# A routed-expert kernel whose router picks experts by eight-largest and index search and gathers tile by tile

## The reference

```python
g_logits = xt @ w_rg + b_rg                       # 4 groups
g_sel = jnp.argmax(g_logits, axis=-1)
e_logits = (xt @ w_re + b_re).reshape(T, 4, 8)    # 8 experts in each group
e_sel = e_logits[chosen group]
top_p, top_i = lax.top_k(softmax(e_sel), 2)       # two experts per token
y = sum over the two experts of  weight * (silu(xt @ w_gate[e]) * (xt @ w_up[e])) @ w_down[e]
```

## Time and profile before

| | us |
|---|---|
| median of 3 runs | 1901.54 |
| lowest and highest run | 1900.3, 1905.17 |
| profiled execution: span from first to last instruction | 1899.8 |
| PE matmul busy | 1538.8 (81%) |
| DVE busy | 424.5 (22%) |
| ACT busy | 248.6 (13%) |
| POOL busy | 86.5 (5%) |
| read from memory | 708.17 MB, 373 GB/s over the span |

### The profile page before, as it was taken

One profiled execution on the slowest core, in us unless ns is written; L12 is line 12 of the kernel. 1 busy time (PEld: TensorE's weight loads), 2 busy tenths in 40 slices (PEclk: granted clock), 3 DMA queues, 4 the chain that ended last, 5 costly groups with the idle time before them and its releaser, 6 DMA issues.

```text
span 1899.8 us, 23382 instructions
## 1 busy us (share of the span) xinstructions
PE 1538.8 (81%) x10250; PEld 744.4 (39%) x10250; DVE 424.5 (22%) x940; ACT 248.6 (13%) x531; POOL 86.5 (5%) x142
## 2 busy tenths in 40 slices
PE   8999777999998778989977677776799667677776
PEld 4654433764454434445522212221355222222222
DVE  3341011326431213464500000000043000000001
ACT  0410000126212011154100000000011000000000
POOL 1100000201100000112100000000000000000000
PEclk9999888999999999999998878888899888788888
DMA  7579999769979999299699999999988999999997
GB/s 289 208 283 423 422 423 417 285 251 388 352 301 417 420 421 413 92 364 381 262 424 424 424 424 423 424 424 424 420 336 333 424 423 423 423 424 424 423 423 293
DMA packets 132110, 711.11 MB, mean 374 GB/s; under 512 B 8376, under 2 KB 13480, under 8 KB 67488
## 3 DMA queue, kind: packets, MB, share of 16 engines
q1 hardware_dynamic: 125584, 697.14, 90.0%
q0 software_dynamic: 4320, 9.78, 1.5%
q10 hardware_dynamic: 2096, 2.57, 0.4%
HBM read 708.17 MB, written 1.05 MB: 373 GB/s over the span
## 4 chain that ended last, share of the span: by engine, by line
PE 45%; DMA 43%; DVE 5%; SPq 2%; issue 2%; ACT 2%; POOL 1%; DVEq 0%; PEldq 0%; ACTq 0%; POOLq 0%
DMA ring<-in_moe_w 25%; DMA ring<-in_moe_w_down 6%; PE pa L824 5%; DMA work<-in_moe_w 5%; PE pb L795 4%; PE pa L842 4%; DMA mod<-in_moe_w 3%; PE acc L897 3%; PE pb L772 3%; PE acc L1425 3%; PE acc L1420 2%; PE pb L750 2%; SPq L706 2%; PE acc L1143 2%; PE acc L1321 2%; DMA ring<-in_moe_w_up 2%
## 5 line engine op out<-in xcount | busy, mean ns | idle before, releaser
L795 PE MATMUL pb<-ring,XT 128*32 128x512 f32 x1296 | 263.1, 742 | 89.5 <-DMA ring<-in_moe_w 89.5
L824 PE MATMUL pa<-ring,work 128*32 128x512 f32 x928 | 182.9, 723 | 71.4 <-DMA ring<-in_moe_w 45.7
L795 PEld LDWEIGHTS pb<-ring,XT 128*32 128x32 f32 x1296 | 59.2, 130 | 242.6 <-DMA ring<-in_moe_w 130.0
L943 DVE TENSOR_TENSOR work<-work,pb 128x256 f32<-128x256 f32 (+1 forms) x32 | 17.7, 554 | 585.5 <-PE pb L795 412.6
L897 PE MATMUL acc<-XT,work 128*128 128x512 f32 x256 | 118.4, 605 | 32.5 <-DVE XT L959 19.6
L842 PE MATMUL pa<-work,HM 128*128 128x128 f32 x1024 | 127.5, 286 | 15.5 <-issue 15.5
L842 PEld LDWEIGHTS pa<-work,HM 128*128 128x128 f32 x1024 | 126.1, 202 | 30.2 <-issue 30.2
L795 PE MATMUL pb<-work,XT 128*32 128x512 f32 x416 | 106.3, 713 | 28.3 <-DMA work<-in_moe_w 28.3
L772 PE MATMUL pb<-ring,XT 128*32 128x256 f32 x1472 | 102.9, 399 | 13.6 <-DMA ring<-in_moe_w_up 13.6
L824 PEld LDWEIGHTS pa<-ring,work 128*32 128x32 f32 x928 | 40.4, 128 | 177.0 <-issue 75.7
L906 ACT COPY XT<-pa 128x512 f32<-128x512 f32 x32 | 18.8, 586 | 588.6 <-PE pa L842 588.6
(11 more groups left out here) (417 smaller groups left out, 1834.5 us busy)
## 6 DMA issues: line engine op xcount, KB each, us to landing
ring<-in_moe_w SPq DMA_DIRECT2D x135, 2048.0 KB
work<-in_moe_w SPq DMA_DIRECT2D x46, 2048.0 KB
ring<-in_moe_w_up SPq DMA_DIRECT2D x28, 2048.0 KB
ring<-in_moe_w_gate SPq DMA_DIRECT2D x26, 2048.0 KB
ring<-in_moe_w_down SPq DMA_DIRECT2D x24, 2048.0 KB
ring<-in_w_mod SPq DMA_DIRECT2D x48, 1024.0 KB
mod<-in_moe_w SPq DMA_DIRECT2D x11, 2048.0 KB
work<-in_moe_w_down SPq DMA_DIRECT2D x8, 2048.0 KB
```

The lines of the kernel that those rows point to most:

```text
L795: last = nc.tensor.matmul(hbank[m][j * CAP:(j + 1) * CAP, :], m_xg[:, k, j * CAP:(j + 1) * CAP], slot_of(s0 + j // 2)[:, at:at + fn], star ...
L824: last = nc.tensor.matmul(pa[j * CAP:(j + 1) * CAP, h, :], m_ht[:, c, j * CAP:(j + 1) * CAP], slot_of(i)[:, at:at + 512], start=(c == 0), ...
```

## The change

In the router each tile's choice takes `max` (the eight largest of a row, in order) and `max_index` (their positions): once for the group, on 8 columns of which 4 are padding of -3e30, and once for the two experts. The logits' columns change places (experts first, then groups). The order of work changes: after tile 0's choice PE computes its ranks, DVE its slots, and PE gathers tile 0 for round 0 while DVE chooses for tile 1; then come tile 1's ranks and slots, and round 0 starts with the second half of its gather. The expert counts are summed after that. Ten warming matmuls before the ranks and four behind become four before each tile's ranks. Tile 1's residual (`carry_tensor(pe, ph, 1)`) moves from behind the logits into round 0, between gate and up and the wait for `hh`. A semaphore of the second mixer is folded into another.

```diff
-            for lo, hi, n in ((0, NG, "g"), (NG, NG + NE, "e")):
+            if ph.moe:
+                pool.wait_ge(assign_ready, TT * ph.moe)
+            for lo, hi, n in ((NE, NE + NG, "g"), (0, NE, "e")):
...
-            carry_tensor(pe, ph, 1)
-            warm_tensor(pe, pb[:, 0, :], 10)
-            pe.wait_ge(assign_ready, ph.moe + 1)
-
-            nc.tensor.matmul(pb[:, 0, 0:NE], before[:, :], m_a[:, 0, :], start=True, stop=True)
-            nc.tensor.matmul(pb[:, 0, NE:2 * NE], before[:, :], m_a[:, 1, :], start=True, stop=False)
-            nc.tensor.matmul(pb[:, 0, NE:2 * NE], ones[:, :], m_a[:, 0, :], start=False, stop=True)
-            nc.tensor.matmul(pb[:, 1, 0:NE], ones[:, :], m_a[:, 0, :], start=True, stop=False)
-            nc.tensor.matmul(pb[:, 1, 0:NE], ones[:, :], m_a[:, 1, :], start=False, stop=True).then_inc(ranks_done, 1)
-            warm_tensor(pe, pa[:, 0, :], 4)
+            n = TT * ph.moe
+            warm_tensor(pe, pb[:, 0, :], 4)
+            pe.wait_ge(assign_ready, n + 1)
+            nc.tensor.matmul(pb[:, 0, 0:NE], before[:, :], m_a[:, 0, :], start=True, stop=True).then_inc(ranks_done, 1)
+            nc.tensor.matmul(pb[:, 1, 0:NE], ones[:, :], m_a[:, 0, :], start=True, stop=False)
+            pe.wait_ge(first_slots, ph.moe + 1)
+            gather_tensor(pe, ph, 0)
+            warm_tensor(pe, pb[:, 0, :], 4)
+            pe.wait_ge(assign_ready, n + 2)
+            nc.tensor.matmul(pb[:, 1, 0:NE], before[:, :], m_a[:, 1, :], start=False, stop=True).then_inc(ranks_done, 1)
+            for t in range(TT):
+                last = nc.tensor.matmul(pb[:, 0, 0:NE], ones[:, :], m_a[:, t, :], start=(t == 0), stop=(t == TT - 1))
+            last.then_inc(ranks_done, 1)
+
+        def gather_tensor(pe, ph, tt):
...
+            for k in range(KC):
+                last = nc.tensor.matmul(xg_ps[:, k, :], HM[:, tt, k * P:(k + 1) * P], m_p[:, tt, :],
+                                        start=(tt == 0 and k % (KC // 2) == 0), stop=(tt == TT - 1), skip_group_check=True)
+                if tt == TT - 1 and k % (KC // 2) == KC // 2 - 1:
+                    last.then_inc(R[0]["gathered"], 1)
...
+            link(v.memset(m_log[:, :, NE + NG:], 3 * NEG))
+
+            def biased(t):
+
+                dve.wait_ge(logits_done, n + t + 1)
+                link(v.tensor_tensor(m_log[:, t, 0:NE + NG], pa[:, t, 0:NE + NG], br[:, :], ALU.add))
+
+            def choice(t):
+
+                g, x = m_g[2][:, t, :], m_lm[:, t, :]
+                link(v.max(m_top[:, 0, t, :], groups[:, t, :]))
+                link(v.max_index(m_at[:, 0, t, :], m_top[:, 0, t, :], groups[:, t, :]))
+                link(v.tensor_tensor(g, order[:, 0:NG], bc(m_at[:, 0, t, 0:1], [P, NG]), ALU.not_equal))
+                link(v.scalar_tensor_tensor(x.rearrange("p (g e) -> p g e", g=NG), bc(g.unsqueeze(2), [P, NG, EPG]), NEG,
+                                            le[:, t, :].rearrange("p (g e) -> p g e", g=NG), ALU.mult, ALU.add))
+                link(v.max(m_top[:, 1, t, :], x))
+                link(v.max_index(m_at[:, 1, t, :], m_top[:, 1, t, :], x))
+                link(v.tensor_tensor(m_o[:, :, t, :], bc(order[:, :].unsqueeze(1), [P, 2, NE]), bc(m_at[:, 1, t, 0:2].unsqueeze(2), [P, 2, NE]), ALU.is_equal))
+                v.tensor_tensor(m_a[:, t, :], m_o[:, 0, t, :], m_o[:, 1, t, :], ALU.add).then_inc(assign_ready, 1)
+                dve.wait_ge(assign_ready, n + t + 1)
+
+            def slots(t):
+
+                dve.wait_ge(ranks_done, 3 * ph.moe + t + 1)
+                link(v.scalar_tensor_tensor(m_rank[:, t, :], pb[:, t, 0:NE], 1.0, m_a[:, t, :], ALU.add, ALU.mult))
+                return v.tensor_tensor(m_p[:, t, :].rearrange("p (j s) -> p j s", j=SIDE), bc(iota[:, :].unsqueeze(1), [P, SIDE, CAP]),
+                                       bc(m_rank[:, t, 0:SIDE].unsqueeze(2), [P, SIDE, CAP]), ALU.is_equal)
...
+            biased(0)
+            choice(0)
+            biased(1)
+            dve.wait_ge(R[0]["gathered"], 2 * ROUNDS * ph.moe + START)
+            slots(0).then_inc(first_slots, 1)
+            choice(1)
+            v.tensor_tensor(m_g[1], lg, bc(m_top[:, 0, :, 0:1], [P, TT, NG]), ALU.subtract).then_inc(rexp_in, 1)
+            v.tensor_tensor(m_s[:, 4, :], m_top[:, 1, :, 1], m_top[:, 1, :, 0], ALU.subtract).then_inc(rexp_in, 1)
+            slots(1).then_inc(R[0]["p_ready"], 1)
...
 # in overfull_vector
+            dve.wait_ge(ranks_done, 3 * (ph.moe + 1))
+            link(v.tensor_reduce(extra_f[:, 2:3], pb[:, 0, 0:NE], AX.X, ALU.max))
...
 # in round_tensor
+            if g == 0 and whole:
+                gather_tensor(pe, ph, 1)
...
+            if whole and g == 0:
+                carry_tensor(pe, ph, 1)
             pe.wait_ge(r["hh_ready"], t + 1 + START)
```

More of the change, by code:

```diff
@@ L17 @@
 I32 = mybir.dt.int32
+U32 = mybir.dt.uint32
 ALU = mybir.AluOpType
@@ L528, in build_model @@
         m_yg = XT[:, :, P:TOK]
-        m_log = area.take(TT, 4 + NE)
+        m_log = area.take(TT, NE + 8)
         m_rank = area.take(TT, NE)
@@ L532, in build_model @@
         m_a = area.take(TT, NE)
-        m_t = [area.take(TT, NE) for _ in range(4)]
+        m_lm = area.take(TT, NE)
+        m_o = area.take(2, TT, NE)
+        m_top = area.take(2, TT, 8)
+        m_at = area.take(2, TT, 8).bitcast(U32)
         m_g = [area.take(TT, NG) for _ in range(3)]
@@ L544, in build_model @@
         logits_done, ranks_done = sem("logits_done"), sem("ranks_done")
+        first_slots = sem("first_tile_slots_ready")
         down_half = sem("first_half_summed")
@@ L625, in router_vector @@
             v = nc.vector
[L627 to L637, removed]
@@ L639, in router_vector @@
-            dve.wait_ge(wr_loaded, 96 * (ph.moe + 1))
[L640 to L654, removed]
@@ L655, in router_vector @@
-            last.then_inc(assign_ready, 1)
-            dve.wait_ge(assign_ready, ph.moe + 1)
-            link(v.tensor_tensor(o2, m_a, o1, ALU.subtract))
-            v.tensor_tensor(m_g[1], lg, bc(gmax.unsqueeze(2), [P, TT, NG]), ALU.subtract).then_inc(rexp_in, 1)
-            v.tensor_tensor(dif, l2, l1, ALU.subtract).then_inc(rexp_in, 1)
-            dve.wait_ge(ranks_done, ph.moe + 1)
-            link(v.scalar_tensor_tensor(m_rank, pb[:, 0, 0:2 * NE].rearrange("p (t e) -> p t e", t=TT), 1.0, m_a,
-                                        ALU.add, ALU.mult))
+            le, lg, groups = m_log[:, :, 0:NE], m_log[:, :, NE:NE + NG], m_log[:, :, NE:]
@@ L667, in weights_vector @@
             gw, w1, w2, dif = (m_s[:, i, :] for i in (3, 5, 6, 4))
-            o1, o2 = m_t[1], m_t[2]
+            o1, o2 = m_o[:, 0], m_o[:, 1]
             dve.wait_ge(rexp_out, 2 * ph.moe + 2)
@@ L837, in round_tensor @@
             pe.wait_ge(r["y_copied"], 2 * t + START)
-            if fn == FN1:
+            if g == 0 and whole:
+                gather_tensor(pe, ph, 1)
+            elif fn == FN1:
                 pe.wait_ge(by_run, TT * (ph.narrow + 1))
-            for k in range(KC):
+            for k in range(0 if g == 0 and whole else KC):
                 for tt in range(TT):
@@ L925, in round_vector @@
             gated = m_pw.rearrange("p t (j s) -> p t j s", j=SIDE)
-            v.tensor_tensor(one, bc(iota[:, :].unsqueeze(1).unsqueeze(1), shape),
-                            bc(m_rank[:, :, ex].unsqueeze(3), shape), ALU.is_equal).then_inc(r["p_ready"], 1)
+            if r is R[1] or g:
+                v.tensor_tensor(one, bc(iota[:, :].unsqueeze(1).unsqueeze(1), shape),
+                                bc(m_rank[:, :, ex].unsqueeze(3), shape), ALU.is_equal).then_inc(r["p_ready"], 1)
             dve.wait_ge(r["p_ready"], t + 1 + START)
@@ L1068, in tables_pool @@
             link(g.tensor_copy(order[:, :], iota_i[:, :]))
-            link(g.tensor_scalar(order[:, :], order[:, :], 64.0, None, ALU.subtract))
+            link(g.tensor_scalar(order[:, :], order[:, :], 1.0, None, ALU.subtract))
             link(g.tensor_copy(thresh[:, :], iota_i[:, 0:MAXPASS - 1]))
@@ L2156, in build_model @@
         assert area.at <= 5120
-        n_cleared = sem("nsa_cleared")
         n_first, n_qps, n_qcp, n_kcp, n_ftr, n_hcp, n_htps, n_htcp = (sem(n) for n in (
@@ L2227, in nsa_pool @@
                                         pattern=[[P, TT], [-CS, NB]], channel_multiplier=1).then_inc(n_opened, 1)
-            nc.gpsimd.memset(n_e, 0.0).then_inc(n_cleared, 1)
+            nc.gpsimd.memset(n_e, 0.0).then_inc(n_opened, 1)
             gain_pool(pool, ph.ln, a["ln1_g"][ph.layer], a["ln1_b"][ph.layer])
@@ L2400, in nsa_vector @@
             v.tensor_copy(n_vc[0:CAP + NB, :, :], pb[0:CAP + NB, 1, SD:3 * SD].rearrange("p (g e) -> p g e", g=SG)).then_inc(n_ccp, 1)
-            dve.wait_ge(n_opened, 4)
-            dve.wait_ge(n_cleared, 1)
+            dve.wait_ge(n_opened, 5)
             def heads(g):
```

5 lines of the change are left out of this document (3 added, 2 removed).

## The result

Twenty runs of the changed kernel have a median of 1905.80 us (1902.35 to 1909.26), twenty of the kernel before 1902.16 us (1899.6 to 1905.64). The ratio is 1.0017, with a 95% interval of 1.0010 to 1.0023: slower by 0.17%, some 3.6 us. That is inside the 0.3% that I had called the same, but it is on the other side of no change than the forecast, which said 4.1 us faster. The profiled execution (1906.26 us itself) has a span 4.7 us longer than the one before.

What follows compares the result with a forecast made beforehand. The saturated weight DMA stream bounds the kernel, stopping once in each router, so earlier first expert matmuls count. 1.23 + 0 + 1.45 + 1.45 = 4.1 us off 1901.5 gives 1897.4 us; range 1892 to 1905.5.

Steps and rivals of the forecast that it cites:

- the other edits: Remaining edits of the diff, such as ones matmuls, overfull count and dropped semaphore: no cost; DMAs and queue places unchanged.
- A, C and D: First, third and fourth mixtures of experts (MoEs): the stream hides the moved carry; gains 1.23, 1.45 and 1.45 us.
- The chain through PE in A: First MoE's router: PE sets the pace; both tiles' slots ready at 128.62 in place of 129.70, 1.08 us earlier.
- The ups: First expert (gate and up) matmuls, which restart the weight stream: 1.23 us earlier in the first MoE, from 133.75.
- The hold-up of the transposes: First MoE's router: the 0.15 us by which the gather still held up PE's transposes goes as well.
- PE idle before the transposes: Router, behind the gather: PE waits about 1.6 us for DVE's 13 small instructions, which are late next.
- C and D: Routers of the third and fourth MoEs: slots 1.40 us earlier plus 0.05 for the transposes, 1.45 us each.
- B gets nothing: Second MoE: loads depend on round 1, so the carry's 1.2 us delay on PE cancels the 1.23 us gain.
- The searches: MAX and MAX_INDEX in each tile's choice: 0.25 us per instruction, 2.1 us a choice, hidden behind PE's work.
- rival of dear searches: Searches at 0.69 us each make the choices overrun: net 4.3 us slower, 1905.8 us; chance 8%.
- The clock rival: TensorE's clock falls in PE's idle times around the gather, before the first expert matmuls: 4.9 us slower, 1906.4; 7%.
- DVE's count decides: Router: DVE's instruction count sets the pace, 2.7 us off each MoE less the second's carry: 9.6 us, 1891.9; 8%.

Runs made afterwards that it cites:

- the experiments on the kernel before alone: Two runs: kernel before with 8 or 32 unused floats (32 or 128 bytes) ahead of the lent weight slots; 1907.98 us (1.0035) and 1908.73 us (1.0031).
- The first experiment: Changed kernel with scratch array m_s 8 floats shorter, so the lent weight slots start where they did before the change; 1899.14 us, ratio 0.9982.
- the late count: Changed kernel, all weight slots on multiples of 256 bytes, four of five overfull-count instructions moved behind the weighted one-hots; 1884.21 us, ratio 0.9897.

## Why the prediction was wrong

The sum of the router was near what the experiments show for it, and the sign was wrong by a term that was not in it.

**The step that failed** is the sentence on the other edits, "No DMA is added, and none changes its place in its queue", and what I made of it: that the saturated stream moves at the same rate before and after, so that an earlier start is an earlier end. The place in the queue is unchanged, but the place in memory is not. I read the diff for instructions, waits and queues, and passed over the sizes of the buffers. The 32 bytes are in it: the logits' 8 columns where there were 4. The missing term is 424 against 421 GB/s in A, C and D. It is 5 to 7 us by the experiments on the kernel before alone (1.0035 and 1.0031), 7 us between the change (3.6 us slower than before) and the same kernel with the slots given back (3.5 us faster), and 8.5 us in the ledger, which is the roughest of the three. With 5 to 7 us the forecast of 4.1 us faster would have been 1 to 3 us slower; 3.6 were measured. The first experiment, which takes only that term out, has the sign and nearly the size of the forecast.

Step by step, what stands of the rest:
- *The chain through PE in A.* The gather at 125.03 (forecast 124.99), the second warming 126.92 (126.76), tile 1's slots at 128.67 (128.62). The ups came 1.08 us earlier, not 1.23. The hold-up of the transposes did go: from the end of DVE's weighting to the ups it is 0.42 us (132.25 to 132.67), where it was 0.63 (133.12 to 133.75). What I had wrong is that DVE's chain is unchanged. From the slots' end to the weighting's end it takes 3.58 us (128.67 to 132.25), where I carried over 3.42: its first instruction now stands 0.21 us behind the slots.
- *PE idle before the transposes*: 1.53 us, forecast 1.6. DVE's small instructions are late next, as said; the late count showed that almost 1 us of them needn't be.
- *C and D*: 1.31 and 1.39 us, forecast 1.45.
- *B gets nothing*: right, by the mechanism named. Against B's logits the up comes 1.06 us earlier and the load behind the dip does not (0.04).
- *The searches*: a choice takes 1.9 us (120.68 to 122.56), forecast 2.1. MAX8 takes 0.16 to 0.20 us, the index search 0.25 to 0.27 in its two instructions together, where I had taken 0.25 for each of four. So the rival of dear searches falls. By the count of the Trainium skill (Vector Engine (DVE) Microarchitecture Reference, 3.9) the search is two instructions, and the rows show two. The load of values takes 0.09 us and not the 0.2 that I had put on it, so my estimate of 2.6 us by that count was too high.
- *The clock rival*: the granted clock is 1.00 in 128 to 134, with idle times of 0.5 and 1.53 us in or around it. It fell.
- *DVE's count decides*: not in the new order, where DVE waits 0.95 and 1.12 us for PE. But I had not asked what the search would be worth in the old one. There it is had in all four MoEs, 9 us with the six warmings gone, near the 9.6 that this rival was priced at for the new order. How that splits was not tried, but the rows of before give an estimate: with its ten warmings, 20 passes of 0.11 us from 124.84, PE is ready for the ranks at 127.06 in A and waits for the choices until 127.68. So the search alone could bring 0.6 us in A and B, by the same rows 0.9 in C and D, some 3 us in all. The other 5 to 6 are the warmings, which can go only because the choices no longer end as late.

## What to carry to other kernels

When a kernel is bound by a saturated stream, read a diff for the addresses of the stream's targets too: any buffer whose size changes ahead of them is an edit of its own, and a term of the sum. Put the targets of large loads on multiples of 256 bytes before anything else is tuned; here it took no instruction and gave 11 us, while the whole rebuilding of the router gave 3 to 4. Starts other than 0, 32 and 128 bytes past a multiple were not tried. And of an edit that changes both the work and its order, run the work in the old order before crediting the order.

## What the hardware showed that was not expected

- Packets of 8192 bytes into SBUF take 309.5 ns in the mean if every target starts on a multiple of 256 bytes, and 314.4 if all start 32 or 128 bytes past one (1000 to 1350 us); this core's saturated rate is 427 against 421 GB/s.
- The eight largest of 8 or 32 columns take 0.16 to 0.20 us and their positions 0.25 to 0.27: hardly more than a plain operation of that size (0.19 for a TENSOR_TENSOR on 32).
- Leaving out eight warming passes on PE between two stretches of work changed the granted clock nowhere in A's router: 1.00 over 122 to 134 us with them and without.
